# Two mixers of a 256-token network: zero-filled queries, gates and output products with tokens on the partitions, tanh gates on ScalarE

## The chip, the cores and the metric

One core of one Trainium2 chip runs the whole program. The metric is the device time of one execution in microseconds (us). Engines: PE is TensorE, DVE is VectorE, ACT is ScalarE, POOL is GpSimd, SP is SyncE, which here issues the weight loads.

## The reference

256 tokens of width 1024 in fp32 pass through two halves of two layers each. The change touches the mixer that stands in the middle of each of the last two layers:

```python
u = rms_norm_2(h, norm_mix[i])
q, k, v, c, g = jnp.split(u @ w_in[i], splits, axis=-1)   # 512, 128, 128, 1024, 2048
q = rms_norm_2(q.reshape(B, S, 8, 64), q_norm[i])
k = rms_norm_2(k.reshape(B, S, 2, 64), k_norm[i])
y_attn = window_attention(q, k, v, sink[i], rel_bias) @ w_attn_out[i]
c_val, c_gate = jnp.split(c, 2, axis=-1)
c = depthwise_conv(c_val * jax.nn.sigmoid(c_gate), conv_w[i], conv_b[i])   # 31 taps
c = jax.nn.silu(layer_norm_2(c, conv_ln_g[i], conv_ln_b[i]))
y_conv = c @ w_conv_out[i]
g_attn, g_conv = jnp.split(jax.nn.sigmoid(g), 2, axis=-1)
h = h + (g_attn * y_attn + g_conv * y_conv) @ w_o[i]
```

Before and after the mixer stand feed-forward layers (1024 to 2 x 2816 and back), which the change does not touch.

## The kernel before

Activations lie as [feature, token]: 128 features on the partitions, 256 tokens in the free dimension. The weights come as a stream of blocks of 128x2048 (1 MB), in a ring of four slots. SP loads a block (L402), ACT rounds it to fp32r as `whi` (`split_hi`, L480), DVE writes the remainder as `wlo` (`split_lo`, L1102), and PE multiplies in three products: hi x hi, hi x lo, lo x hi (`mm3`, L1985). Each engine's queue is written out by hand and runs in order; all ties between engines are semaphores. A slot is loaded again when PE's `blk_done` says that its block is done.

`window(l)` is the mixer, and each engine has its own function of this name (ACT L937, DVE L1771, PE L2502). Its 24 blocks are:

- blocks for q (2), k, v; after them six fp32 matmuls take the mean square of each head (L2518), ACT forms the inverse root (L966 Ln, L971 Exp), DVE scales q and k (L1822) in six instructions.
- twelve blocks j = 0 to 11: 0 to 3 the convolution's values and gates, 4 to 7 the first gate `g_attn`, 8 to 11 `g_conv`. PE does block j into one of two banks of `ab` (`a_block`, L1999, 48 matmuls with 256 columns), then `attend` for head j - 1 (L2381): scores (L2393) of head j - 1, transposes (L2402) of head j - 2, values (L2421) of head j - 3. I call this a round.
- DVE in round j takes the bank with 1/rms of the tokens applied (`scaled_evac`, L1509), splits the weight block j + 2, finds the row maximum of the scores (`top`, L1659), forms 1/sum (`normal`, L1673) and does 6 or 7 convolution taps, each in two instructions (L1792).
- ACT in round j splits block j + 2, scales the exponentials of head j - 2 by 1/sum (L835, PE's transposes wait for this), then takes the exponentials of head j - 1 (L844) and copies transposed ones (L858). In rounds 1 and 3 it takes a sigmoid of the convolution's gate (L975). The other gates are sigmoids of 2048 columns at once (L982, L987).
- two blocks of `w_attn_out` and two of `w_conv_out` (`b_block`, L2084: 48 matmuls with 256 columns, weights stationary, result as [feature, token] in the four banks of `acc`). Within the first stands the matmul for the convolution's variance (L2541). DVE multiplies the banks by the gates (L1864, L1881), adds the two (L1883), ACT rounds the sum (L1013) and DVE writes its remainder (L1876).
- four blocks of `w_o`, the last two together (`b_last`, L2104), which need the split of both.

`window_attention`'s queries of two heads share a tile, so that a head's queries and keys take 64 of 128 partitions (L2522). `qk` gives per head and query block one fp32 product, which PE runs as two instructions, and two fp32r products with the position bias (L2523 to L2525).

## Time and profile before

| | |
|---|---|
| runs | 2342.78 us median of 3 (2340.3 to 2346.83) |
| profiled execution | span 2338.6 us from first to last instruction; what lies around it is not in the profile |
| PE | 2249.4 us busy, 96% |
| DVE | 1761.8 us, 75% |
| ACT | 1191.4 us, 51% |
| POOL | 236.7 us, 10% |
| chain that ended last | PE 79%, DVE 11%, ACT 5%, DMA 3% |
| DMA | 202 GB/s mean |
| mean granted TensorE clock | 0.990 |

The first mixer lies at about 1344 to 1526 us, the second at about 1934 to 2116. In a timeline a row gives the start, how long until the last of its instructions ended, the engine, the line, output and inputs, shape and count; a bracket gives the idle time before it and who ended it. A matmul's own time contains its way through the array, so that successive ones overlap: the distance of starts is what a matmul costs.

### The profile page before, as it was taken

To read this page: it belongs to the slowest core of one execution; us is meant where nothing else is said; L and a number is where in the kernel's file an instruction comes from. 1 tells how busy PE (TensorE), PEld (TensorE's weight loads), DVE (VectorE), ACT (ScalarE), POOL (GpSimd) and SP (SyncE) were. 2 spreads that over 40 slices of the span, in tenths; PEclk is the share of its full clock that TensorE was granted. 3 is DMA by queue.
4 is the path that set the end of the run, shared out by engine and by line. 5 is a ranking of instruction groups with operands and counts; after the bars stand their busy time and mean duration, and the time that the engine had idled before them with its cause. 6 is when DMAs were issued, how large, how long until landed. Compare 5 with 4: busy or idle time off the path is not lost.

```text
span 2338.6 us, 36936 instructions
## 1 busy us (share of the span) xinstructions
PE 2249.4 (96%) x14724; PEld 2036.4 (87%) x14724; DVE 1761.8 (75%) x1858; ACT 1191.4 (51%) x1293; POOL 236.7 (10%) x199
## 2 busy tenths in 40 slices
PE   7999889999999989999999999999999999999999
PEld 7997889788889877788788998988998899898899
DVE  6898786788789985868677569877577746987755
ACT  3444645455455445555455455655455545565544
POOL 0122000001111300000022000012002200001200
PEclk9999999999999999999999999999999999999999
DMA  9996434577569852455555443455545554344553
GB/s 377 359 351 230 164 124 148 203 266 291 217 257 360 309 194 96 175 180 217 188 183 194 162 162 109 163 181 196 180 170 182 192 180 152 117 146 180 188 188 131
DMA packets 75935, 471.49 MB, mean 202 GB/s; under 512 B 8708, under 2 KB 8964, under 8 KB 27581
## 3 DMA queue, kind: packets, MB, share of 16 engines
q1 hardware_dynamic: 53136, 383.80, 45.2%
q0 software_dynamic: 18976, 68.71, 7.8%
q10 hardware_dynamic: 3724, 17.57, 2.0%
q8 instruction: 74, 1.21, 0.2%
q14 instruction: 25, 0.20, 0.0%
HBM read 468.98 MB, written 1.06 MB: 201 GB/s over the span
## 4 chain that ended last, share of the span: by engine, by line
PE 79%; DVE 11%; ACT 5%; DMA 3%; issue 2%; ACTq 0%; DVEq 0%; SPq 0%
PE ab L1992 19%; PE acc L1992 13%; PE acc L2133 11%; PE mb L2025 10%; PE ab L2025 10%; PE mb L2027 5%; PE ab L2027 5%; DVE wlo L1102 3%; ACT whi L480 2%; PE mb L2393 2%; DMA sc<-start 1%; DMA modmem<-mods 1%; DMA raw<-stream 1%; DVE sc L1792 1%; DVE sc L1241 1%
## 5 line engine op out<-in xcount | busy, mean ns | idle before, releaser
L1102 DVE TENSOR_TENSOR wlo<-raw,whi 128x2048 fp32r<-128x2048 f32 x361 | 832.6, 2310 | 245.2 <-ACT whi L480 242.6
L480 ACT ACTIVATE whi<-raw 128x2048 fp32r<-128x2048 f32 x361 | 689.3, 1911 | 414.0 <-DMA raw<-stream 292.0
L1992 PE MATMUL ab<-uu,whi 128*128 128x256 f32 x3104 | 576.4, 288 | 17.4 <-DVE wlo L1102 8.3
L1992 PEld LDWEIGHTS ab<-uu,whi 128*128 128x128 f32 x3104 | 492.8, 195 | 27.8 <-issue 15.4
L1992 PE MATMUL ab<-uu,wlo 128*128 128x256 f32 x1552 | 443.7, 286 | 0.0
L2025 PE MATMUL ab<-uu,whi 128*128 128x512 f32 x1056 | 374.8, 398 | 8.3 <-DVE uu L1453 5.3
L2025 PE MATMUL mb<-uu,whi 128*128 128x512 f32 x1056 | 375.0, 398 | 3.5 <-DVE wlo L1102 2.1
L1992 PEld LDWEIGHTS ab<-uu,wlo 128*128 128x128 f32 x1552 | 302.7, 195 | 0.0
L1992 PE MATMUL acc<-h_hi,whi 128*128 128x256 f32 (+1 forms) x1032 | 293.4, 284 | 4.4 <-ACT sc L916 1.6
L2027 PE MATMUL ab<-uu,wlo 128*128 128x256 f32 x1056 | 295.6, 280 | 0.0
L2027 PE MATMUL mb<-uu,wlo 128*128 128x256 f32 x1056 | 295.3, 280 | 0.0
L1992 PE MATMUL acc<-h_lo,whi 128*128 128x256 f32 (+1 forms) x1032 | 292.0, 283 | 0.0
L1992 PE MATMUL acc<-h_hi,wlo 128*128 128x256 f32 (+1 forms) x1032 | 292.0, 283 | 0.0
L2025 PEld LDWEIGHTS ab<-uu,whi 128*128 128x128 f32 x1056 | 199.1, 188 | 57.4 <-issue 8.6
L2025 PEld LDWEIGHTS mb<-uu,whi 128*128 128x128 f32 x1056 | 198.8, 188 | 53.5 <-DVE wlo L1102 3.6
L454 POOL TENSOR_TENSOR sc<-sc,rstd 128x512 f32<-128x512 f32 x44 | 120.3, 2733 | 959.2 <-ACT sc L699 959.2
L1992 PEld LDWEIGHTS acc<-h_hi,whi 128*128 128x128 f32 x1032 | 197.4, 191 | 6.2 <-DVE h_lo L1876 2.0
L2027 PEld LDWEIGHTS ab<-uu,wlo 128*128 128x128 f32 x1056 | 200.0, 189 | 0.0
L2027 PEld LDWEIGHTS mb<-uu,wlo 128*128 128x128 f32 x1056 | 199.7, 189 | 0.1
L1992 PEld LDWEIGHTS acc<-h_lo,whi 128*128 128x128 f32 x1032 | 197.4, 191 | 0.1
L1992 PEld LDWEIGHTS acc<-h_hi,wlo 128*128 128x128 f32 x1032 | 197.4, 191 | 0.0
L435 POOL DMA_DIRECT2D modmem<-mods x128 | 68.5, 536 | 939.6 <-DVE sc L1238 658.8
(355 smaller groups left out, 2832.4 us busy)
## 6 DMA issues: line engine op xcount, KB each, us to landing
raw<-stream SPq DMA_DIRECT2D x365, 1024.0 KB, 4.8
modmem<-mods POOLq DMA_DIRECT2D x128, 512.0 KB, 6.0
sc<-lnrows ACTq DMA_DIRECT2D x5, 1024.0 KB, 4.8
sc<-start ACTq DMA_DIRECT2D x4, 1024.0 KB, 16.5
gateb<-gaterows ACTq DMA_DIRECT2D x6, 512.0 KB, 3.8
hank<-toep POOLq DMA_DIRECT2D x8, 192.0 KB, 4.0
x<-xT ACTq DMA_DIRECT2D x1, 1024.0 KB, 27.3
x<-xn ACTq DMA_DIRECT2D x1, 1024.0 KB, 8.8
```

The source lines that it names most:

```text
L435: pool.dma_start(modmem[:, i % MODRING, :], mods[i]).then_inc(mod_in[i % MODRING], 16)
L454: nc.gpsimd.tensor_tensor(gated, gated, r, ALU.mult).then_inc(g2_ready, 1)
L480: nc.scalar.activation(whi[:, n % RAW, :], raw[:, n % RAW, :], ACT.Copy).then_inc(hi_ready, 1)
L1102: nc.vector.tensor_tensor(wlo[:, n % RAW, :], raw[:, n % RAW, :], whi[:, n % RAW, :].bitcast(F32), ALU.subtract).then_inc(lo_ready, 1)
L1241: nc.vector.scalar_tensor_tensor(out=out, in0=part, scalar=cact[:, k:k + 1], in1=out, op0=ALU.mult, op1=ALU.add).then_inc(mod_done, 1)
L1792: ins = nc.vector.scalar_tensor_tensor(out=sc[:, 28 + c, :], in0=cpad[:, c, t:t + T], scalar=w, in1=sc[:, 28 + c, :], op0=ALU.mult, op1=AL ...
L1992: ins = nc.tensor.matmul(out, l, r, start=first and i == 0, stop=last and i == 2, skip_group_check=True)
L2025: nc.tensor.matmul(bank[:, m, :].rearrange("p (a t) -> p a t", a=2), wh[:, k, m * P:m * P + P], uu[:, :, k, :], start=k == 0, stop=k == DM ...
L2027: ins = nc.tensor.matmul(bank[:, m, 0:T], wl[:, k, m * P:m * P + P], u_hi[:, k, :], start=False, stop=k == DM - 1, skip_group_check=True)
L2133: ins = nc.tensor.matmul(acc[:, 2 * t + c, :], l, w[:, k, 512 * c:512 * c + 512], start=first and k == 0 and w is wh and l is hh, stop=las ...
L2393: ins = nc.tensor.matmul(mb[:, k % 2, o:o + w], l, r, start=(c == 0), stop=(c == len(terms) - 1), skip_group_check=True)
```

## The change

1. Queries: DVE writes them into `qpad`, eight tiles of all 128 partitions in the memory of `h_hi`, of which POOL has set everything to zero before; the other head's half stays zero, and the product uses all rows.
2. The gate blocks j = 4 to 11 are done with u stationary (`t_block`), so that the result is [token, feature], and ACT takes it from the bank with tanh, whose scale is half of 1/rms as a column. sigmoid(x) = (1 + tanh(x/2))/2; the 1 is added where DVE multiplies, the half goes into the residual's factor (0.5 for 1.0). The convolution's gates are tanh too.
3. The four blocks of output products are done with the activations stationary and 512 weight columns moving (`quarters`, 24 matmuls a block).
4. The sum of the two, now [token, feature], is turned on PE by 16 transposes in two lots (`turn`), and ACT and DVE take its parts from PSUM.
5. Ln and Exp of the head norms use one table set, and waits on own semaphores become `link`.

```diff
@@ POOL
             for l in range(DEPTH):
                 ffn(4 * l)
+                pool.wait_ge(u_ready, 32 + 16 * l)
+                nc.gpsimd.memset(qpad[:], 0.0).then_inc(qpad_zero, 1)
                 ffn(4 * l + 2)
@@ ACT, window
+                nc.scalar.activation(small[:, 10:12], mb[:, 0, 0:2], ACT.Copy, scale=0.5).then_inc(rcol_ready, 1)
...
                     if j == 0:
+                        nc.scalar.preload_act_table_set("natural_log_exp_and_others")
...
                     elif j in (1, 3):
                         act.wait_ge(bank_evac[a[0] % 2], a[0] // 2 + 1)
-                        nc.scalar.activation(gated, gated, ACT.Sigmoid).then_inc(csig_ready, 1)
+                        nc.scalar.activation(gated, gated, ACT.Tanh, scale=0.5).then_inc(csig_ready, 1)
+                    elif j >= 4:
+                        done(g[0])
+                        i, c = (j - 4) // 4, (j - 4) % 4
+                        for t in range(2):
+                            ins = nc.scalar.activation(gates(i)[:, t, T * c:T * c + T], ab[:, a[0] % 2, t * T:t * T + T],
+                                                       ACT.Tanh, scale=small[:, 10 + t:11 + t])
+                        ins.then_inc(bank_evac[a[0] % 2], 1)
                     tick()
                     if j >= 1:
                         attend(8 + 8 * l, j - 1, 1.0, l)
-                    if j == 9:
...
-                        nc.scalar.activation(sc[:, 0:8, :], sc[:, 0:8, :], ACT.Sigmoid).then_inc(sig_ready, 1)
...
-                gate_sigmoids()
                 split_hi(g[0] + 1 + AHEAD)
                 for q in range(4):
-                    act.wait_ge(comb_ready, 4 * l + q + 1)
-                    nc.scalar.activation(h_hi[:, 8 + 2 * q:10 + 2 * q, :], sc[:, 2 * q:2 * q + 2, :], ACT.Copy)\
+                    act.wait_ge(combt_ps, 4 * l + q + 1)
+                    nc.scalar.activation(h_hi[:, 8 + 2 * q:10 + 2 * q, :], v2(combt(q)), ACT.Copy)\
                         .then_inc(combhi_ready, 1)
@@ DVE, window
-                    else:
-                        scaled_evac(sc[:, 2 * (j - 4):2 * (j - 4) + 2, :])
...
-                        for i in range(6):
...
+                        for b in range(2):
+                            r = slice(64 * b, 64 * b + 64)
+                            ins = nc.vector.scalar_tensor_tensor(out=padded[r, :, b, :], in0=sc[r, 16:20, :],
+                                                                 scalar=small[r, 0:1], in1=sc[r, 32:36, :],
+                                                                 op0=ALU.mult, op1=ALU.mult)
...
+                comb(0)
+                comb(1)
+                comb(2)
+                comb_lo(0)
+                comb_lo(1)
+                comb(3)
+                comb_lo(2)
                 comb_lo(3)
@@ PE, window
                 def qk(h, qb):
-                    r = slice(64 * (h % 2), 64 * (h % 2) + 64)
-                    return [(sc[r, 16 + h // 2, qb * P:qb * P + P], sc[r, 20 + h // 4, :], 0, T),
+                    return [(qpad[:, h, qb * P:qb * P + P], sc[:, 20 + h // 4, :], 0, T),
...
                 for j in range(1, 12):
-                    a_static(1)
+                    if j < 4:
+                        a_static(1)
+                    else:
+                        t_block()
...
+                def turn(c):
+                    pe.wait_ge(comb_ready, 4 * l + 2 * c + 2)
+                    for m in range(4 * c, 4 * c + 4):
+                        for t in range(2):
+                            ins = nc.tensor.transpose(combt(m // 2)[:, T * (m % 2) + P * t:T * (m % 2) + P * t + P],
+                                                      gates(0)[:, t, P * m:P * m + P], ident)
+                        if m % 2:
+                            ins.then_inc(combt_ps, 1)
+
+                quarters(g[0], 0, True, False, None, lambda q: variance() if q == 3 else None)
+                quarters(g[0] + 1, 2, False, True)
...
+                quarters(g[0] + 2, 4, True, False, (m1_ready, 4 * l))
...
+                quarters(g[0] + 3, 6, False, True, None, lambda q: turn(0) if q == 3 else None)
 
                 for i in range(2):
                     pe.wait_ge(comblo_ready, 4 * l + i + 1)
...
+                    if i == 0:
+                        turn(1)
```

How it moves instructions. ACT, a round of the gate blocks (L835 or L849 is the scaling that PE's transposes wait for, L844 or L858 the exponentials, L858 or L872 the copy), before:

```order
L480 ACTIVATE whi<-raw 128x2048
L835 ACTIVATE sc<-sc,small 128x256 x2
L844 ACTIVATE sc,small<-mb,small 128x256 x2
L848 ACTIVATE small<-small,par 128x2
L858 ACTIVATE sc<-acc 128x512
```

and now:

```order
L494 ACTIVATE whi<-raw 128x2048
L994 ACTIVATE sc<-ab,small 128x256 x2
L849 ACTIVATE sc<-sc,small 128x256 x2
L858 ACTIVATE sc,small<-mb,small 128x256 x2
L862 ACTIVATE small<-small,par 128x2
L872 ACTIVATE sc<-acc 128x512
```

The two gate functions (L994), which wait for the round's block, stand ahead of the scaling.

DVE, from the three weight splits behind the first gate products to the next weight splits (L1881 or L1893 multiplies, L1883 or L1895 adds, L1876 or L1899 writes the remainder), before:

```order
L1102 TENSOR_TENSOR wlo<-raw,whi 128x2048 x3
L1881 TENSOR_TENSOR sc<-acc,sc 128x512
L1883 TENSOR_TENSOR sc<-sc 128x512
L1881 TENSOR_TENSOR sc<-acc,sc 128x512
L1883 TENSOR_TENSOR sc<-sc 128x512
L1876 TENSOR_TENSOR h_lo<-sc,h_hi 128x512
L1881 TENSOR_TENSOR sc<-acc,sc 128x512
L1883 TENSOR_TENSOR sc<-sc 128x512
L1876 TENSOR_TENSOR h_lo<-sc,h_hi 128x512
L1881 TENSOR_TENSOR sc<-acc,sc 128x512
L1883 TENSOR_TENSOR sc<-sc 128x512
L1876 TENSOR_TENSOR h_lo<-sc,h_hi 128x512 x2
```

and now:

```order
L1112 TENSOR_TENSOR wlo<-raw,whi 128x2048 x3
L1893 SCALAR_TENSOR_TENSOR sc<-sc,acc 128x512
L1895 TENSOR_TENSOR sc<-sc 128x512
L1893 SCALAR_TENSOR_TENSOR sc<-sc,acc 128x512
L1895 TENSOR_TENSOR sc<-sc 128x512
L1893 SCALAR_TENSOR_TENSOR sc<-sc,acc 128x512
L1895 TENSOR_TENSOR sc<-sc 128x512
L1899 TENSOR_TENSOR h_lo<-ab,h_hi 128x512 x2
L1893 SCALAR_TENSOR_TENSOR sc<-sc,acc 128x512
L1895 TENSOR_TENSOR sc<-sc 128x512
L1899 TENSOR_TENSOR h_lo<-mb,h_hi 128x512 x2
L1112 TENSOR_TENSOR wlo<-raw,whi 128x2048 x3
```

The first remainder stands behind the third sum, and the last two, which read transposed parts, stand right ahead of the next splits.

PE, the end of the second `w_conv_out` block (L2155) and the start of the first `w_o` block (L2014), now:

```order
L2155 MATMUL acc<-wlo,h_hi 128x512
L2155 MATMUL acc<-whi,h_lo 128x512
L2583 MATMUL ab<-par,sc 128x128 x8
L2155 MATMUL acc<-whi,h_hi 128x512
L2155 MATMUL acc<-wlo,h_hi 128x512
L2155 MATMUL acc<-whi,h_lo 128x512
L2155 MATMUL acc<-whi,h_hi 128x512
L2155 MATMUL acc<-wlo,h_hi 128x512
L2155 MATMUL acc<-whi,h_lo 128x512
L2014 MATMUL acc<-h_hi,whi 128x256
```

Eight transposes (L2583) have come in ahead of the last quarter; eight more follow the first `w_o` block.

## Rows read from the trace of the kernel before

**Rows 1.** The page, part 1: busy time, share, instructions.

```profile
PE 2249.4 (96%) x14724; PEld 2036.4 (87%) x14724; DVE 1761.8 (75%) x1858; ACT 1191.4 (51%) x1293; POOL 236.7 (10%) x199
```

**Rows 2.** Timeline, PE, one round: start us, us, engine, line, tiles, form.

```profile
1433.12 0.70 PE L2393 MATMUL mb<-sc 64*128 64x256 f32 x2
...
1435.14 0.60 PE L2402 MATMUL acc<-par,sc 128*128 128x128 f32 x4
1435.67 1.08 PE L2421 MATMUL acc<-sc 128*64 128x256 f32 x4
1436.68 0.51 PE L1992 MATMUL ab<-uu,whi 128*128 128x256 f32 x2
...
1442.63 0.70 PE L2393 MATMUL mb<-sc 64*128 64x256 f32 x2
```

**Rows 3.** Timeline, DVE: first and last of the five rounds 4 to 8.

```profile
1414.57 0.68 DVE L1512 TENSOR_TENSOR sc<-ab,rstd 128x512 f32<-128x512 f32 x1
...
1447.10 2.46 DVE L1792 SCALAR_TENSOR_TENSOR sc<-sc,par 128x256 f32<-128x256 f32 x6
...
1462.69 0.68 DVE L1512 TENSOR_TENSOR sc<-ab,rstd 128x512 f32<-128x512 f32 x1
```

**Rows 4.** Timeline, ACT, one of those rounds.

```profile
1447.23 0.47 ACT L844 ACTIVATE sc<-mb,small 128x256 f32<-128x256 f32 x1 [5.23 <-DVE small L1663]
...
1450.62 0.90 ACT L835 ACTIVATE sc<-sc,small 128x256 f32<-128x256 f32 x2
```

**Rows 5.** Timeline, ACT, DVE and PE, from the head norms to head 1.

```profile
1378.45 1.28 ACT L971 ACT_TABLE_LOAD   x1
1381.45 1.67 DVE L1822 SCALAR_TENSOR_TENSOR sc<-sc,small 128x256 f32<-128x256 f32 x4
1383.97 0.95 PE L2393 MATMUL mb<-sc 64*128 64x256 f32 x2 [1.68 <-DVE sc L1822]
1394.92 0.69 DVE L1512 TENSOR_TENSOR sc<-ab,rstd 128x512 f32<-128x512 f32 x1 [1.48 <-PE ab L1992]
1406.58 0.66 PE L2402 MATMUL acc<-par,sc 128*128 128x128 f32 x4 [1.28 <-ACT sc L835]
1478.51 1.21 DVE L1842 SCALAR_TENSOR_TENSOR sc<-mb,sc 128x1024 f32<-128x1024 f32 x1
```

**Rows 6.** Stretches: engine busy times, granted clock (third number from the end), DMA.

```profile
855.80:859.80 4.00, 3.94 (x33) 3.97 (x34) 3.90 (x6) 3.56 (x5) 0.00 (x0) 1.00 0.43 128
871.30:875.30 4.00, 3.96 (x22) 3.96 (x23) 3.96 (x3) 0.00 (x0) 0.00 (x0) 0.62 0.38 158
...
1384.00:1391.00 7.00, 7.00 (x26) 5.54 (x27) 6.62 (x14) 4.63 (x9) 0.00 (x0) 0.52 0.33 136
```

**Rows 7.** Timeline, PE: two long waits, the first right behind eight transposes.

```profile
852.77 1.20 PE L2260 MATMUL acc<-par,x 128*128 128x128 f32 x8 [0.39 <-DVE x L1401]
855.86 0.36 PE L1992 MATMUL ab<-uu,whi 128*128 128x256 f32 x1 [1.89 <-DVE uu L1357]
...
871.34 0.51 PE L1992 MATMUL ab<-uu,whi 128*128 128x256 f32 x2 [2.88 <-DVE wlo L1102]
```

**Rows 8.** Timeline, PE: 512-column matmuls, then fp32 ones at full height.

```profile
933.13 0.62 PE L2133 MATMUL acc<-whi,h_hi 128*128 128x512 f32 x2
...
1373.80 1.89 PE L2518 MATMUL mb<-sc,par 128*128 128x256 f32 x8
```

**Rows 9.** Timeline, PE, DVE and ACT, from the convolution's variance to the last blocks.

```profile
1482.05 0.70 PE L2541 MATMUL mb<-sc,mean_r 128*128 128x256 f32 x2 [1.21 <-DVE sc L1846]
1489.10 1.28 DVE L1864 TENSOR_TENSOR sc<-acc,sc 128x512 f32<-128x512 f32 x2
1492.10 4.49 DVE L1102 TENSOR_TENSOR wlo<-raw,whi 128x2048 fp32r<-128x2048 f32 x2
1502.47 0.38 PE L1992 MATMUL acc<-h_hi,whi 128*128 128x256 f32 x1 [0.80 <-DVE h_lo L1876]
1506.24 3.71 ACT L480 ACTIVATE whi<-raw 128x2048 fp32r<-128x2048 f32 x2
```

More of the change, by code:

```diff
@@ L1856, in window @@
                 ph[0] += 1
-                dve.wait_ge(sig_ready, 6 * l + 1)
-                for q in range(4):
+                for b in range(2):
+                    dve.wait_ge(bank_evac[b], a[0] // 2)
+                for q, (t, c) in enumerate(QUARTERS):
                     if q % 2 == 0:
@@ L1863, in window @@
                     acc_wait(q)
-                    ins = nc.vector.tensor_tensor(sc[:, 2 * q:2 * q + 2, :], v2(acc[:, q, :]), sc[:, 2 * q:2 * q + 2, :],
-                                                  ALU.mult)
-                    ins.then_inc(m1_ready, 1)
+                    part = gates(0)[:, t, 512 * c:512 * c + 512]
+                    nc.vector.scalar_tensor_tensor(out=part, in0=part, scalar=1.0, in1=acc[:, 2 * t + c, :],
+                                                   op0=ALU.add, op1=ALU.mult).then_inc(m1_ready, 1)
                 split_lo(g[0] - 1 + AHEAD)
@@ L1871, in window, with comb @@
                 ph[0] += 1
-                dve.wait_ge(sig_ready, 6 * l + 2)
+                def comb(q):
+                    t, c = QUARTERS[q]
+                    part, other = [gates(i)[:, t, 512 * c:512 * c + 512] for i in range(2)]
+                    acc_wait(q)
+                    link(nc.vector.scalar_tensor_tensor(out=other, in0=other, scalar=1.0, in1=acc[:, 2 * t + c, :],
+                                                        op0=ALU.add, op1=ALU.mult))
+                    nc.vector.tensor_tensor(part, part, other, ALU.add).then_inc(comb_ready, 1)
                 def comb_lo(q):
                     dve.wait_ge(combhi_ready, 4 * l + q + 1)
-                    nc.vector.tensor_tensor(h_lo[:, 8 + 2 * q:10 + 2 * q, :], sc[:, 2 * q:2 * q + 2, :],
+                    nc.vector.tensor_tensor(h_lo[:, 8 + 2 * q:10 + 2 * q, :], v2(combt(q)),
                                             h_hi[:, 8 + 2 * q:10 + 2 * q, :].bitcast(F32), ALU.subtract).then_inc(comblo_ready, 1)
-                for q in range(4):
-                    acc_wait(q)
-                    link(nc.vector.tensor_tensor(sc[:, 8 + 2 * q:10 + 2 * q, :], v2(acc[:, q, :]),
-                                                 sc[:, 8 + 2 * q:10 + 2 * q, :], ALU.mult))
-                    nc.vector.tensor_tensor(sc[:, 2 * q:2 * q + 2, :], sc[:, 2 * q:2 * q + 2, :],
-                                            sc[:, 8 + 2 * q:10 + 2 * q, :], ALU.add).then_inc(comb_ready, 1)
-                    if q:
-                        comb_lo(q - 1)
+                comb(0)
[5 more added lines that the diff above has]
+                comb_lo(2)
                 comb_lo(3)
@@ L2541, in variance, with quarters @@
                     nc.tensor.matmul(mb[:, 1, 0:T], meanones, sc[:, 36, :], start=True, stop=True).then_inc(cvar_ps, 1)
-                b_block(g[0], h_hi, h_lo, 0, None, True, False, None, variance)
-                b_block(g[0] + 1, h_hi, h_lo, 2, None, False, True)
+                def quarters(n, i, first, last, taken=None, before=None):
+                    split_ready(n)
+                    for q, (t, c) in enumerate(QUARTERS):
+                        if before is not None:
+                            before(q)
+                        if taken is not None:
+                            pe.wait_ge(taken[0], taken[1] + q + 1)
+                        ins = group(n, h_hi, h_lo, i, t, (c,), first, last)
+                        if last and q < 3:
+                            ins.then_inc(acc_done, 1)
+                    ins.then_inc(blk_done, 1)
@@ L2546, in window @@
+                quarters(g[0] + 1, 2, False, True)
                 pe.wait_ge(clo_ready, 2 * l + 1)
-                b_block(g[0] + 2, h_hi, h_lo, 4, None, True, False, (m1_ready, 4 * l))
+                quarters(g[0] + 2, 4, True, False, (m1_ready, 4 * l))
                 pe.wait_ge(clo_ready, 2 * l + 2)
-                b_block(g[0] + 3, h_hi, h_lo, 6, None, False, True)
+                for b in range(2):
+                    pe.wait_ge(bank_evac[b], a[0] // 2)
+                quarters(g[0] + 3, 6, False, True, None, lambda q: turn(0) if q == 3 else None)
```

53 lines of the change are left out of this document (28 added, 25 removed).

## The prediction

> **What bounds the kernel now.** I read the page's shares first: PE is busy 96% of the span [rows 1], and the chain that ended last is mostly PE. So only PE's own work and its few waits count. Then I went through the timelines of PE, DVE and ACT over the first of the two mixers (1344 to 1526 us) and compared the second: its waits on PE are the same ones, of 1.7, 1.3, 1.2 and 0.8 us. All that follows is worked for one mixer and doubled.
>
> In the middle stage PE does one block of the input product and one head per round. A round takes 9.51 us: 2.02 us for the scores, 0.53 for the transposes, 1.01 for the values and 5.95 for the block with its switches [rows 2]. The block has 48 matmuls, so 0.12 us each. DVE is as full as PE: its five rounds 4 to 8 take 48.1 us, 9.62 each, with no idle time [rows 3]. ACT has time: the scaling of a head's exponentials ends at 1451.5 [rows 4], before the block behind which PE wants them is done. The reader is to see that two engines pace this stage, so that taking work from one gives what the other allows, and that ACT, which has slack, is about to get work in a place where PE waits for what is behind it.
>
> **Up to head 2.** The head norms lose a table load of 1.28 us between Ln and Exp. DVE's six products of 256 columns (four take 1.67 us, so 0.4 each, 2.4 in all) become one of 512 and two of 1024 elements per row; a 1024-element product took 1.21 us and issues the next after 1.13, so 2.86 in all [rows 5]. Net: PE's wait of 1.68 us [rows 5] shrinks by 0.8. It is followed now by a stretch of 7 us at a granted clock of 0.52, near the lower of the two levels, 1.2 GHz [rows 6], which makes the second block 3.4 us late, and DVE waits 1.48 us for it [rows 5]. With a wait of 0.9 us and scores that use all rows I take the clock to stay up. DVE then runs on, 0.8 + 1.5 = 2.3 us earlier. That is all this part can give, because head 1's scaling on ACT stands behind a gate function that waits for DVE's fourth evacuation (the 1.28 us wait at 1406.58 [rows 5]). PE, which is faster now, waits there some 4.3 us instead of 1.3. After an idle time of 2.88 us [rows 7] the clock was 0.62 over 4 us [rows 6]; I take the clock to fall at 4.3 us, for 1.7 to 3.4 us, most likely 2.3. **This part: 0**, between -2.3 (no fall) and +1.1.
>
> **Rounds 4 to 8.** Full-height queries replace 64-row ones. Fp32 matmuls at full height issue every 0.216 us (1.89 us for eight, less the last one's 0.38 [rows 8]). A head has four of these and four at 0.12, 1.34 us, and some 0.1 for the switch of format: 1.44 for 2.02. A bound from the other side is nothing saved. The zero rows cost no time of their own; the zeroing is one POOL instruction after 1350 us, where POOL is idle, and its result is needed at 1381. Gates as [token, feature] keep 48 matmuls of 256 columns, so 0.12 us each as before. DVE loses an evacuation of 0.60 us a round, so 9.0 is its pace. But ACT now has, behind its wait for the block, two tanh of 256 columns (an exponential of 256 took 0.47 us [rows 4]; I estimate 0.8 for both, as they overlap) and only then the scaling of the head before (two in 0.90 us [rows 4]), for which PE's transposes wait. From the block's end: 0.2 + 0.8 + 0.9 = 1.9 us, where the scores end after 1.44. So PE waits 0.5 a round, and a round is 1.9 + 0.53 + 1.01 + 5.86 = 9.3. **Five rounds: -1.0**, between -2.5 (DVE's pace) and 0.
>
> In round 9 there are no scores to hide it: PE waits the whole 1.9 us at head 7's transposes, where it waited for nothing. **+1.9**, at least +0.5.
>
> A rule speaks against the first term. In the trace, two 64-row fp32 matmuls take 0.63 us to the next instruction [rows 2], and two at full height 0.43 [rows 8]. The Trainium skill, "TensorE: Matmul & The Clock Gate", section "Step-by-step: what each phase is for", says that a weight load's time goes by columns and that the number of rows does not matter. By that rule the padding would save nothing, and the five rounds would be worth about 0 and not -1.0. The two rows differ with it, and I go by the rows.
>
> **Convolution's variance.** After block 11 PE had the mean (0.6 us) and 36 matmuls of 0.12 to do and then waited 1.21 us [rows 9]: 6.1 us. DVE's last evacuation leaves that chain, but two tanh (0.2 + 0.8) and a weight split (1.9, half of the row at 1506.24 [rows 9]) now stand before ACT's square, which takes 1.1, and DVE's two sums, 1.1: 5.1 us. **-1.0.** From there to the end of DVE's first product at 1489.8 (the row at 1489.10 [rows 9]) the chain goes through ACT and DVE as before, so that the 0.3 us that each block of 24 matmuls of 512 columns saves (0.62 less 0.39 = 0.227 us each [rows 8], 5.44 for 5.76) is not seen here.
>
> **The sum and its transpose.** Counting from that first product's end at 1489.8: DVE has 2.4 us of products and 6.6 of splits (two in 4.49 [rows 9]), then two sums of 1.32 us: done at +11.7. PE has done its block and three quarters of the next at +9.6, so it waits 2.1 us for the sums, then does eight transposes (0.53 for four [rows 2], 1.06) and the last quarter, 1.4. The first output block starts at +14.2; it started at 1502.47, +12.7 [rows 9]. **+1.5.** The wait of 0.80 there [rows 9] goes. Behind that block stand eight more transposes, 1.2 us with the switch. ACT's last two copies wait for them, and the two weight splits that stood at 1506.24 [rows 9] now stand behind the copies. From the block's end: copies done at 1.8 (0.7 for four transposes, then 0.55 each), first split at 3.7, DVE's two splits of 2.2 behind it at 8.15. PE, after 1.2 and a block of 5.76, is there at 6.9. PE waits 1.25 more. **+2.4.**
>
> **Sum:** 0 - 1.0 + 1.9 - 1.0 + 1.5 + 2.4 = +3.8 us a mixer, +8 us in all. Against the profiled span of 2338.6 us that is 2346.6. The median of the runs lies 4.2 over this span, so I forecast 2351 us. A measurement can tell about 0.3%, 7 us. With the bounds above, this case reaches from 2345 to 2355.
>
> **Rivals.**
> *The stalls are smaller and the kernel stays level* (25%): rounds at DVE's 9.0 us, no fall of the clock after the 4.3 us wait. For it: falls don't follow every wait; an idle 1.89 us behind eight transposes [rows 7] left the clock at 1.00 [rows 6]. Against: 4.3 us is longer than any wait inside the trace. Per mixer -2.3 - 1.5 from the sum, 0: 2343 us.
> *Faster: PE's savings go through* (14%). If DVE's rounds can be absorbed by the two spare banks and ACT's tanh is early enough, each mixer keeps 0.6 x 8 of the scores, 1.3 of the wide blocks and the 3.4 us of the lost clock, less 2.1 of transposes: -7.4, so 2328 us. It decides if PE isn't held at head 1's transposes. Against it: DVE without idle time [rows 3].
> *Slower still: the clock falls at the sum, too* (21%). The wait of 2.1 us stands right before eight transposes. A mixer loses 1.7 to 3.4 us there, and perhaps as much at round 9's wait: 2355 to 2361. The rows are divided: 0.62 after 2.88 us of idle, 1.00 after transposes and 1.89 [rows 6, 7]. The Trainium skill, same page, section "Part 4: PE-mode transpose", says that transposes don't count as work for the clock; by this rule the fall here is sure.
> *The change doesn't do what it says* (under 2%, in the first rival): the order of PE's instructions shows it does.
>
> **How the numbers follow.** Forecast 40%, level 25%, slower still 21%, faster 14%. Slower by over 0.3% is above 2350: 60% of the forecast and the third rival, 0.45. Faster is 0.15, the rest is same. For 8 in 10 the range leaves out the faster case and the top of the third rival: 2338 to 2358.
>
> **What would show it.** Steps right: a PE wait of about 4 us for ACT's scaling before head 1's transposes with a clock under 1 after it; waits of about 0.5 us in rounds 4 to 8 and 1.9 in round 9, all on that line; 2 us before the first eight transposes, released by DVE's sum; 1.2 us before the last two blocks, released by DVE's split. Wrong: rounds of 9.0 us or less, no wait before the transposes of the sum, or a mixer (first block to last) shorter than now.

## The result and the profile after

| | before | the change |
|---|---|---|
| median of 18 runs each | 2342.97 us | 2352.0 us |
| ratio | 1 | 1.0032 (95%: 1.0025 to 1.0040) |
| profiled execution, span | 2338.6 us | 2350.7 us |
| from the head norms to the end of the last `w_o` block, first and second mixer | 151.8, 151.8 us | 154.8, 157.5 us |

The change makes the kernel slower by 9 us. The last line is taken from PE's timeline: from the first `headones` matmul (L2518, now L2540) to the first matmul behind the mixer. I call it the mixer's length; every experiment below is judged by it first, because the code outside the mixers, which is the same, differs by some us from execution to execution. Of the 12.1 us between the two profiled spans 3.0 and 5.6 lie in the mixers, 1.3 ahead of them and 2.1 between them, where every matmul of 110 us took a little longer. A profile of another execution of the changed kernel has 156.7 and 156.8 us. The mean of the four is 156.45, so 4.6 us a mixer, 9.3 in all: this accounts for the medians.

The page's first part shows PE as busy as before [rows 1], and DVE and ACT relieved by 6 and 11 us:

```profile
PE 2248.5 (96%) x14564; PEld 2034.6 (87%) x14564; DVE 1756.0 (75%) x1836; ACT 1180.5 (50%) x1311; POOL 240.3 (10%) x201
```

The time is in waits. Timeline of the changed kernel, PE, first mixer (start us, us, engine, line, tiles, form; in brackets the idle time before the row and what ended it):

```profile
1384.80 0.70 PE L2415 MATMUL mb<-sc,qpad 128*128 128x256 f32 x2 [1.18 <-DVE qpad L1835]
...
1391.99 0.60 PE L2415 MATMUL mb<-sc,qpad 128*128 128x256 f32 x2
...
1393.33 0.60 PE L2424 MATMUL acc<-par,sc 128*128 128x128 f32 x4
...
1405.69 1.11 PE L2424 MATMUL acc<-par,sc 128*128 128x128 f32 x4 [4.68 <-ACT sc L849]
...
1416.60 0.66 PE L2424 MATMUL acc<-par,sc 128*128 128x128 f32 x4 [0.39 <-ACT sc L849]
...
1425.94 0.66 PE L2424 MATMUL acc<-par,sc 128*128 128x128 f32 x4 [0.39 <-ACT sc L849]
...
1463.22 0.66 PE L2424 MATMUL acc<-par,sc 128*128 128x128 f32 x4 [1.72 <-ACT sc L849]
...
1482.63 0.70 PE L2565 MATMUL mb<-sc,mean_r 128*128 128x256 f32 x2 [0.31 <-DVE sc L1861]
...
1502.07 1.09 PE L2583 MATMUL ab<-par,sc 128*128 128x128 f32 x8 [1.75 <-DVE sc L1895]
...
1518.33 0.36 PE L2014 MATMUL acc<-h_hi,whi 128*128 128x256 f32 x1 [1.41 <-DVE wlo L1112]
```

Against [rows 5, 9] the wait ahead of the first scores is down from 1.68 to 1.18 us, that ahead of the variance from 1.21 to 0.31, and that ahead of the first `w_o` block is gone. Head 1's went from 1.28 to 4.68, and four places are new: 0.39 in each of rounds 4 to 8, 1.72 in round 9, 1.75 at the sum's transposes, 1.41 at the last blocks. A head's scores now take 1391.99 to 1393.33, 1.34 us, against 2.02 [rows 2].

The same stretch on ACT shows who holds PE. L989 is the convolution's gate, L994 the other gates, L849 the scaling for which PE waits:

```profile
1404.21 0.63 ACT L989 ACTIVATE sc<-sc 128x512 f32<-128x512 f32 x1 [2.90 <-DVE sc L1522]
1404.75 0.89 ACT L849 ACTIVATE sc<-sc,small 128x256 f32<-128x256 f32 x2
...
1414.92 0.84 ACT L994 ACTIVATE sc<-ab,small 128x256 f32<-128x256 f32 x2 [3.42 <-PE ab L2014]
1415.65 0.90 ACT L849 ACTIVATE sc<-sc,small 128x256 f32<-128x256 f32 x2
```

ACT is idle for 2.90 and 3.42 us with the scaling's inputs ready (DVE's `normal` had ended at 1400.4), because the gate function stands ahead of it.

Stretches of the changed kernel (busy times of PE, PEld, DVE, ACT, POOL; then granted clock, DMA share, GB/s):

```profile
1404.00:1409.00 5.00, 3.31 (x9) 1.84 (x10) 4.93 (x8) 2.42 (x8) 0.00 (x0) 0.67 0.02 5
1464.00:1468.00 4.00, 4.00 (x30) 3.46 (x29) 3.65 (x7) 2.32 (x2) 0.00 (x0) 1.00 0.48 199
1502.00:1506.00 4.00, 3.93 (x28) 3.68 (x29) 3.88 (x7) 1.09 (x2) 0.00 (x0) 1.00 0.14 16
2099.00:2102.00 3.00, 3.00 (x11) 2.51 (x10) 1.98 (x3) 1.19 (x2) 0.00 (x0) 0.50 0.00 0
```

The fall behind the first scores [rows 6] is gone. The clock falls behind the 4.68 us wait instead, not behind the waits of 1.72 and 1.75 in the first mixer, but behind the second mixer's wait at the sum (1.88 us), to 0.50 over 2099 to 2102.

### The profile page after: what moved, and what is told of

It is laid out like the page before. It is cut to its first block, busy times and chain, and to the rows that moved or that the text cites. A ratio compares the mean times of both kernels' runs of the same rounds, so it can differ in the third digit from the quotient of the medians.

```text
span 2350.7 us, 36614 instructions
## 1 busy us (share of the span) xinstructions
PE 2248.5 (96%) x14564; PEld 2034.6 (87%) x14564; DVE 1756.0 (75%) x1836; ACT 1180.5 (50%) x1311; POOL 240.3 (10%) x201
## 4 chain that ended last, share of the span: by engine, by line
PE 79%; DVE 11%; ACT 5%; DMA 2%; issue 2%; ACTq 0%; DVEq 0%; SPq 0%
PE ab L2014 19%; PE acc L2014 13%; PE acc L2155 13%; PE mb L2047 10%; PE ab L2047 10%; PE mb L2049 5%; PE ab L2049 5%; DVE wlo L1112 3%; ACT whi L494 1%; DMA sc<-start 1%; DMA modmem<-mods 1%; DVE sc L1803 1%; PE acc L2443 1%; DVE sc L1251 1%; PE acc L2424 1%
## 5 line engine op out<-in xcount | busy, mean ns | idle before, releaser
L2014 PE MATMUL ab<-uu,whi 128*128 128x256 f32 x2592 | 479.6, 287 | 17.1 <-DVE wlo L1112 8.3
L2014 PEld LDWEIGHTS ab<-uu,whi 128*128 128x128 f32 x2592 | 411.0, 195 | 21.6 <-issue 10.9
L2014 PE MATMUL ab<-uu,wlo 128*128 128x256 f32 x1296 | 370.2, 286 | 0.0
L2049 PE MATMUL ab<-uu,wlo 128*128 128x256 f32 x1056 | 296.7, 281 | 0.0
L2014 PE MATMUL acc<-h_hi,whi 128*128 (+1 forms) x904 | 256.4, 284 | 5.6 <-DVE wlo L1112 2.8
L2014 PE MATMUL acc<-h_lo,whi 128*128 (+1 forms) x904 | 255.8, 283 | 0.0
L2014 PE MATMUL acc<-h_hi,wlo 128*128 (+1 forms) x904 | 255.8, 283 | 0.0
L2014 PEld LDWEIGHTS ab<-uu,wlo 128*128 128x128 f32 x1296 | 252.5, 195 | 0.0
L2047 PEld LDWEIGHTS ab<-uu,whi 128*128 128x128 f32 x1056 | 199.5, 189 | 57.9 <-issue 8.5
L2049 PEld LDWEIGHTS ab<-uu,wlo 128*128 128x128 f32 x1056 | 200.6, 190 | 0.0
L2014 PEld LDWEIGHTS acc<-h_hi,whi 128*128 128x128 f32 x904 | 173.5, 192 | 7.0 <-issue 3.9
L2155 PE MATMUL acc<-whi,h_hi 128*128 128x512 f32 x512 | 173.0, 394 | 1.6 <-DVE wlo L1112 0.8
L2014 PEld LDWEIGHTS acc<-h_lo,whi 128*128 128x128 f32 x904 | 173.5, 192 | 0.1
L2014 PEld LDWEIGHTS acc<-h_hi,wlo 128*128 128x128 f32 x904 | 173.5, 192 | 0.0
```

Source lines behind the costliest of these rows:

```text
L2014: ins = nc.tensor.matmul(out, l, r, start=first and i == 0, stop=last and i == 2, skip_group_check=True)
L2047: nc.tensor.matmul(bank[:, m, :].rearrange("p (a t) -> p a t", a=2), wh[:, k, m * P:m * P + P], uu[:, :, k, :], start=k == 0, stop=k == DM ...
L2049: ins = nc.tensor.matmul(bank[:, m, 0:T], wl[:, k, m * P:m * P + P], u_hi[:, k, :], start=False, stop=k == DM - 1, skip_group_check=True)
L2155: ins = nc.tensor.matmul(acc[:, 2 * t + c, :], l, w[:, k, 512 * c:512 * c + 512], start=first and k == 0 and w is wh and l is hh, stop=las ...
```

## The experiments

Two theories stood against each other. *ACT's order and the late sum*: PE is held where the prediction has it, by gate functions ahead of the scaling, by the sums and by the late splits. *DVE's pace*: DVE is as full as PE, so a freed wait only comes back as one for DVE.

In the table, parts of a mixer in us, on PE: from the first scores to head 3's; from there to head 7's scores (four rounds); to head 7's transposes; to the variance; the mixer's length. Two figures are the two mixers.

| kernel | to h3 | four rounds | to its transposes | to variance | length | median us, ratio (95%) |
|---|---|---|---|---|---|---|
| before | 30.15 | 38.01 | 9.42 | 20.50 | 151.8 | 2343 |
| the change | 29.92, 30.86 | 37.30 | 11.20 | 19.4 | 154.8, 157.5 | 2352.0, 1.0032 |
| the change, again | 30.21, 30.34 | 37.3 | 11.21 | 20.9 | 156.7, 156.8 | 2354.3, 1.0046 (1.0029 to 1.0062) |
| gates behind | 30.88, 31.12 | 34.9 | 8.73 | 19.4 | 150.9, 151.1 | 2340.5, 0.9988 (0.9978 to 0.9998) |
| conv gate behind | 24.81 | 40.4 | 11.20 | 20.95, 19.43 | 154.4, 152.9 | 2344.1, 1.0011 (1.0000 to 1.0022) |
| both behind | 24.81 | 37.2 | 10.6 | 19.4 | 149.1, 149.0 | 2338.6, 0.9985 (0.9973 to 0.9996) |
| turn early | 30.80, 30.62 | 37.3 | 11.20 | 19.4 | 154.0, 153.8 | 2347.4, 1.0027 (1.0016 to 1.0039) |
| all moves | 24.80 | 37.2 | 10.6 | 19.4 | 145.7, 145.7 | 2332.0, 0.9955 (0.9942 to 0.9968) |
| all moves, again | 24.81 | 37.2 | 10.6 | 19.4 | 145.7, 145.7 | 2331.4, 0.9946 (0.9932 to 0.9960) |
| all moves, 64 rows | 25.66 | 38.0 | 9.42 | 19.4 | 146.1, 146.1 | 2335.5, 0.9974 (0.9960 to 0.9988) |

**Gates behind the scaling** (rounds of j = 4 to 11, on ACT; `mid` takes the two tanh with it):

```diff
-                    elif j >= 4:
-                        done(g[0])
...
                     tick()
-                        attend(8 + 8 * l, j - 1, 1.0, l)
+                        attend(8 + 8 * l, j - 1, 1.0, l, mid)
@@ attend
                     ins.then_inc(p_norm, 1)
+                if mid is not None:
+                    mid()
```

> The changed kernel, with ACT's two gate tanh of a round (j = 4 to 11) issued behind the scaling of the exponentials that PE's transposes wait for. Theory ACT order (the prediction's): the PE waits of 0.39 us in rounds 4 to 8 and of 1.72 us in round 9 go, rounds fall from 9.32 to DVE's pace of about 9.0 us, so 1.6 + 1.7 = 3.3 us a mixer: span about 2344, ratio to before about 1.0005. Rival DVE pace: DVE is the bound already and hands PE a new wait of the same size (for the conv sums or a weight split): under 1 us a mixer, ratio stays at 1.003.

Measured: every 0.39 and the 1.72 are gone, as ACT's order predicts, and nothing on DVE took their place. Timeline of this kernel, PE:

```profile
1406.26 1.12 PE L2432 MATMUL acc<-par,sc 128*128 128x128 f32 x4 [4.68 <-ACT sc L849]
...
1416.25 0.59 PE L2423 MATMUL mb<-sc,qpad 128*128 128x256 f32 x2
...
1424.99 0.60 PE L2423 MATMUL mb<-sc,qpad 128*128 128x256 f32 x2
...
1459.92 0.60 PE L2432 MATMUL acc<-par,sc 128*128 128x128 f32 x4
```

Rounds are 8.74 us (1416.25 to 1424.99), and not DVE's 9.0: PE is late after head 1, so DVE is ahead of it (it waits 1.25 us for PE's scores at 1417.79), and PE runs at its own pace, busy for all of the 52 us from 1408 to 1460. The two parts that this edit touches, the four rounds and the one to head 7's transposes, get shorter by 2.4 and 2.5 us, 4.8 together, not 3.3. This order in ACT's queue alone costs as much as the whole change (4.6). The mixer's length is 5.4 us under the change's mean; the rest lies in the falls of the clock, which differ from mixer to mixer (none here behind round 9 or at the sum, longer ones behind head 1).

**The convolution's gate behind** (the same with j = 3 alone; with j = 1 `mid` is called at once):

```diff
-                    elif j in (1, 3):
-                        act.wait_ge(bank_evac[a[0] % 2], a[0] // 2 + 1)
-                        nc.scalar.activation(gated, gated, ACT.Tanh, scale=0.5).then_inc(csig_ready, 1)
+                    if j in (1, 3):
+                        def mid(ai=a[0]):
+                            act.wait_ge(bank_evac[ai % 2], ai // 2 + 1)
+                            nc.scalar.activation(gated, gated, ACT.Tanh, scale=0.5).then_inc(csig_ready, 1)
```

> The changed kernel, with only the tanh of the convolution's second gate (j = 3) issued behind the scaling of head 1. Theory ACT order: PE's wait of 4.68 us before head 1's transposes shrinks to about 1.2 us, and the granted clock of 0.50 behind it goes; PE gains 3.5 us or more there, but DVE's round 3 (1403.5 to 1413.7, no idle time) does not move, so that only the small rounds' slack is won: 1 to 3 us a mixer. Rival clock: the fall costs most of the loss, and with it gone the mixer gains 4 us or more, ratio at or under 1.000. Rival DVE pace: nothing is won, ratio 1.003, the wait shows up again on a row released by DVE.

PE, first mixer, and two stretches:

```profile
1402.91 0.65 PE L2432 MATMUL acc<-par,sc 128*128 128x128 f32 x4 [1.14 <-ACT sc L849]
1413.83 0.66 PE L2432 MATMUL acc<-par,sc 128*128 128x128 f32 x4 [1.97 <-ACT sc L849]
```

```profile
1401.00:1406.00 5.00, 3.86 (x25) 2.89 (x25) 4.99 (x11) 2.49 (x4) 0.00 (x0) 1.00 0.65 213
1414.00:1418.00 4.00, 4.00 (x19) 3.15 (x19) 3.96 (x7) 0.38 (x2) 0.00 (x0) 0.65 0.21 86
```

The wait is 1.14 us and no fall follows it. The part up to head 3 shrinks by 5.5 us to 24.81, but the four rounds grow by 3.1: head 2 now waits 1.97 us, with a fall of the clock behind it. So 2.8 us a mixer are kept, within the theory's 1 to 3; here neither rival holds. This part also prices the fall after 4.68 us. Without it the part would have been 24.81 + (4.68 - 1.14) = 28.35. The eight mixers with the wait of about 4.7 us have 29.92 to 31.12, mean 30.6: the fall costs 1.6 to 2.8 us, 2.2 in the mean. This takes the part to be the same otherwise.

**Both behind.**

> Both of these orders together (j = 3 to 11). Theory ACT order: DVE sets the pace from round 3 on, 9.0 us a round; at most 1 us a mixer more than the first of them alone gives: 3.3 to 4.3 us a mixer, span 2342 to 2344. Rival clock: the two add up, 7 us or more a mixer, span under 2337.

149.0 us, 7.4 less than the change, and a span of 2333.2: not the 3.3 to 4.3 of the theory, but the 7 and more that I had given the rival, near the sum of the two orders (5.4 + 2.8 = 8.2). I had put too little on the clock: in this kernel no wait inside the rounds is over 1.6 us and the clock does not fall in either mixer of this profile, which neither order alone gave. DVE's pace shows up now: the last rounds are 8.9 to 9.1 us, and heads 1, 2 and 7 wait 1.1 to 1.5 us.

**The turn early** (DVE's third weight split goes behind the fourth sum):

```diff
                 split_lo(g[0] - 1 + AHEAD)
                 split_lo(g[0] + AHEAD)
-                split_lo(g[0] + 1 + AHEAD)
...
                 comb(3)
+                split_lo(g[0] - 1 + AHEAD)
                 comb_lo(2)
```

> The changed kernel with DVE's third weight split moved from ahead of the first sum to behind the fourth. Theory: the sums are no longer late, PE's wait of 1.75 us before the first eight transposes shrinks to about 0.2, and the clock does not fall there in either mixer: 1.6 us a mixer, 3.3 us in all and 1 to 2 us more where the clock fell; ratio 1.001 to 1.002. Rival acc pace: the second sum waits for PE's second quarter anyway, and the wait stays above 1 us, ratio 1.003.

PE's transposes and the DVE row that releases them, this kernel:

```profile
1496.67 1.09 PE L2583 MATMUL ab<-par,sc 128*128 128x128 f32 x8
...
1512.92 0.36 PE L2014 MATMUL acc<-h_hi,whi 128*128 128x256 f32 x1 [1.41 <-DVE wlo L1112]
```

```profile
1493.84 0.69 DVE L1892 SCALAR_TENSOR_TENSOR sc<-sc,acc 128x512 f32<-128x512 f32 x1 [0.45 <-PE acc L2155]
```

No wait is left at the transposes, DVE even waits 0.45 us for PE's first quarter, and from the variance to the first `w_o` block it takes 20.1 us in both mixers for 21.8. The wait of 1.41 at the last blocks is untouched. Both were as expected. The median ratio (1.0027) does not lie clear of the change's two (1.0032 and 1.0046); what the move gives, 1.6 us a mixer, is read from this part alone. The remaining 0.9 us against the change's mean length lies in the falls of the clock, of which none stands behind round 9 or at the sum here.

**All moves**: both orders, the turn early, and the split of the third `w_o` block ahead of the last two copies and remainders:

```diff
@@ ACT
                         .then_inc(combhi_ready, 1)
+                    if q == 1:
+                        split_hi(g[0] + 2 + AHEAD)
...
-                b_blocks(4)
+                b_blocks(4, 1)
@@ DVE
+                split_lo(g[0] + AHEAD)
                 comb_lo(2)
                 comb_lo(3)
-                b_blocks(4)
+                b_blocks(4, None, 1)
```

> Both orders on ACT, and in the output part two moves: DVE's third weight split goes from ahead of the first sum to behind the fourth, and on both engines the split of the third w_o block goes ahead of the last two copies (ACT) and remainders (DVE) of the turned sum. Expected beside what the two ACT orders give: the 1.75 us wait before the first eight transposes shrinks to 0.3, with it the clock fall behind it in the second mixer (1.6 us), and the 1.41 us wait before the last two blocks goes: 2.9 us a mixer and 1.6 once. Theory: 2 x (3.3 to 4.3) + 2 x 2.9 + 1.6 = 14 to 16 us under the change, 2336 to 2338, ratio 0.997 to 0.998: faster than both. Rival DVE pace: DVE's moved splits come late for PE elsewhere, ratio 1.000 or above.

> The version with all four moves once more, beside the one with POOL's taps: 145.7 us a mixer, ratio 0.995 to 0.996, no stretch of a mixer at a granted clock under 0.9.

The last stretch (first `w_o` block to the end) goes from 25.5 to 23.9 us, the one before it from 21.8 to 20.1. All of PE's waits over 0.2 us that are left in the first mixer, and the clock in three stretches of it:

```profile
1384.93 0.70 PE L2426 MATMUL mb<-sc,qpad 128*128 128x256 f32 x2 [1.18 <-DVE qpad L1845]
1402.28 0.66 PE L2435 MATMUL acc<-par,sc 128*128 128x128 f32 x4 [1.14 <-ACT sc L849]
1412.46 0.66 PE L2435 MATMUL acc<-par,sc 128*128 128x128 f32 x4 [1.24 <-ACT sc L849]
1457.56 0.66 PE L2435 MATMUL acc<-par,sc 128*128 128x128 f32 x4 [1.51 <-ACT sc L849]
1476.98 0.70 PE L2576 MATMUL mb<-sc,mean_r 128*128 128x256 f32 x2 [0.31 <-DVE sc L1871]
1484.86 0.47 PE L2166 MATMUL acc<-whi,h_hi 128*128 128x512 f32 x1 [0.33 <-DVE sc L1891]
```

```profile
1375.00:1415.00 40.00, 36.45 (x268) 33.68 (x267) 36.08 (x67) 20.79 (x36) 0.00 (x0) 1.00 0.38 132
1415.00:1470.00 55.00, 53.27 (x391) 47.61 (x390) 54.61 (x117) 31.38 (x64) 0.00 (x0) 1.00 0.31 115
1470.00:1520.00 50.00, 49.22 (x318) 44.22 (x317) 40.85 (x41) 28.15 (x32) 0.00 (x0) 1.00 0.42 148
```

145.7 us in all four mixers of two profiles, 6.1 less than before: with its queues ordered for it, the change makes the kernel 11 us **faster** than before (ratios 0.9955 and 0.9946) and 20 us faster than the change as it was made. I had expected 0.997 to 0.998; the two orders on ACT gave the surplus. In the middle stretch DVE is busy 54.61 of 55 us, PE 53.27.

**64 rows again**, in the changed kernel and in the version with all moves:

```diff
-                    return [(qpad[:, h, qb * P:qb * P + P], sc[:, 20 + h // 4, :], 0, T),
+                    r = slice(64 * (h % 2), 64 * (h % 2) + 64)
+                    return [(qpad[r, h, qb * P:qb * P + P], sc[r, 20 + h // 4, :], 0, T),
```

> The changed kernel with scores over 64 rows again (the queries' 64 rows of the padded tile by the keys' 64), all else as changed. Theory rows as traced: a head's scores take 2.02 us and not 1.34; the first three are hidden in the 4.68 us wait before head 1's transposes, the five in rounds 4 to 8 take up the 0.39 us wait and lengthen the round by 0.3: 1.5 us a mixer, 3 us in all, ratio 1.0045. Rival, the rule that the row count costs nothing: scores stay at 1.34 us and the ratio at 1.003.

> The version with all four moves (149.0 - 3.3 = 145.7 us from the head norms to the mixer's end) with 64-row scores. Theory rows as traced: PE's own round becomes 8.7 + 0.7 = 9.4 us and passes DVE's 9.0, so 0.4 us in each of five rounds and a part of the first three: 2 to 4 us a mixer, 147.7 to 149.7. Rival, the row rule: 145.7 again.

PE in the changed kernel with 64 rows:

```profile
1404.22 0.70 PE L2415 MATMUL mb<-sc,qpad 64*128 64x256 f32 x2
1405.27 0.70 PE L2415 MATMUL mb<-sc,qpad 64*128 64x256 f32 x2
1408.95 1.11 PE L2424 MATMUL acc<-par,sc 128*128 128x128 f32 x4 [2.54 <-ACT sc L849]
```

Half a head's scores take 1.05 us (1404.22 to 1405.27), and a whole head's in a round 2.02, as before, for 1.34 at full height. It is tempting to take this for the price of 64 rows. The trace of the kernel before has short fp32 products in a row, in its first half:

```profile
282.28 1.99 PE L2312 MATMUL acc<-sc 16*128 16x256 f32 x8
...
334.62 1.96 PE L2345 MATMUL acc<-sc 64*128 64x256 f32 x12 [1.21 <-ACT sc L802]
```

Eight with 16 rows take 1.99 us, where eight at full height took 1.89 [rows 8]: the first takes 0.32 us to the next one's start, all others 0.216, as at full height. Twelve with 64 rows, in the two halves of the partitions by turns, take 1.96. So in a run of one height the number of rows costs nothing. The Trainium skill ("TensorE: Matmul & The Clock Gate", "Step-by-step: what each phase is for") says that the number of rows does not matter for a weight load's time. These rows agree with it. The extra time stands where PE goes from one height to another: from a matmul of 128 rows to the first of 16 it is 0.21 us (0.12 between 128-row ones), then the 0.32, and 0.30 from the last 16-row one to the next of 128 and 0.22 behind that. The scores with 64 rows show the same four distances (0.21, 0.32, 0.31, 0.22), in each half of a head, because their 64-row products alternate with the 128-row ones of the position bias. The zero-filled queries save these changes of height.

But little of the 0.7 us arrives. In the changed kernel (155.7 and 157.4 us, the second with three falls of the clock, median 2351.8, ratio 1.0046, 1.0029 to 1.0063) the four rounds go from 37.30 to 38.01, and the first three heads hide in head 1's wait, which shrinks from 4.68 to 2.54 (and to 1.28 in the second mixer, where the clock falls behind the first scores). With all moves, where I expected 2 to 4 us, it is 0.4 a mixer: 0.9 and 0.8 us in the first two parts, of which 1.2 come back at head 7, whose wait of 1.51 is used up. PE's saving on the scores is worth 0.4 us out of 8 x 0.68 = 5.4, because DVE, busy for 87.32 of the 88 us from 1385 to 1473 in the version with all moves, sets the length of this stage. (The medians of the two lie 3.6 us apart, more than the mixers' 0.8; the rest lies outside the mixers and stays open. The profiled span of the 64-row version, 2325.9 us, is even the shorter one.)

**The kernel before, with zero-filled queries alone**, and **with head 1's scaling ahead of the gate besides**:

```diff
+                pool.wait_ge(u_ready, 32 + 16 * l)
+                nc.gpsimd.memset(qpad[:], 0.0).then_inc(kn_ps, 1)
...
-                        for i in range(6):
+                        for b in range(2):
+                            r = slice(64 * b, 64 * b + 64)
+                            ins = nc.vector.scalar_tensor_tensor(out=padded[r, :, b, :], in0=sc[r, 16:20, :],
...
-                    return [(sc[r, 16 + h // 2, qb * P:qb * P + P], sc[r, 20 + h // 4, :], 0, T),
+                    return [(qpad[:, h, qb * P:qb * P + P], sc[:, 20 + h // 4, :], 0, T),
```

> The kernel before with the zero-filled queries alone (POOL's zeroing, DVE's three products for six, full-height scores). Theory two engines pace: scores shrink to 1.34 us, but DVE's rounds of 9.62 us have no idle time, so that PE waits 0.6 us a round for DVE instead: 0 to 1 us a mixer, ratio 0.999 to 1.000. Rival PE pace: 8 x 0.68 = 5.4 us a mixer, ratio 0.995. Rival slower: the products' 0.46 us more on DVE delay the first scores and the fall of the clock behind them lasts longer: up to +1 us a mixer.

> The kernel before with the zero-filled queries, and the sigmoid of the convolution's second gate (j = 3) issued behind head 1's scaling. It tells what the good version (145.7 us a mixer) owes to the order and what to the change itself. Theory DVE pace: before, DVE's work up to the convolution's mean has no idle time but 1.48 us, and its rounds need 9.62 us, so that PE's shorter scores and the freed wait cannot be used: 150 to 152 us a mixer, ratio 0.998 to 1.001. Rival: order and PE's scores are what pays, 147 or less, ratio 0.995.

The first has 152.0 and 154.6 us (median 2349.1, ratio 1.0016, 1.0000 to 1.0032), no gain from 5.4 us less work on PE and rather a loss. PE:

```profile
1385.78 0.70 PE L2402 MATMUL mb<-sc,qpad 128*128 128x256 f32 x2 [2.46 <-DVE qpad L1830]
1406.67 0.55 PE L2411 MATMUL acc<-par,sc 128*128 128x128 f32 x3 [3.18 <-ACT sc L839]
...
1462.60 0.65 PE L2411 MATMUL acc<-par,sc 128*128 128x128 f32 x4 [2.12 <-ACT sc L839]
```

The waits grow to 2.46, 3.18 and 2.12 us, and the clock falls behind the first two in both mixers, behind the third in one: what PE saves it pays in waits and to its clock. With the order mended too (median 2344.7, ratio 1.0009, 0.9998 to 1.0021) the length is 150.7 and 150.6, as DVE's pace has it: DVE is then busy 85.17 of the 86 us from 1387 to 1473. In the second mixer the clock fell behind the 2.46 us wait (0.50 from 1978 to 1981), the next round took 8.71 us for 7.20, and the mixer was no longer for it: PE would have waited for DVE anyway.

So about 1 of the 6.1 us a mixer comes from the queries and the first order. Where the rest lies, in us of the first mixer (before the first scores; the part up to head 3; from there to the variance; from there to the mixer's end):

| kernel | to the first scores | to h3 | h3 to variance | variance to end |
|---|---|---|---|---|
| before | 10.2 | 30.2 | 67.9 | 43.6 |
| before, zero-filled queries and order | 11.0 | 24.8 | 71.4 | 43.6 |
| all moves | 9.7 | 24.8 | 67.3 | 44.0 |

From the second line to the third the head norms, with a table load less, give 1.3, and the stretch that DVE paces, with eight of its evacuations gone, gives 4.1. The output products with 512 columns and the turn give nothing: even with the splits moved, that part is some 0.4 us longer than before. Which share each item has within a part was not tested.

**The change once more.**

> The changed kernel once more: ratio 1.003. For the clock: it falls after the 4.68 us wait before head 1's transposes in both mixers; after the 1.7 to 1.9 us wait before the sum's transposes it falls in both if transposes do not hold it up, and in none or one if what counts there is chance.

Ratio 1.0046, with 1.0032 inside its interval. The clock fell behind head 1's wait and behind round 9's in both mixers, and behind the wait at the sum (1.84 and 1.75 us) in none:

```profile
1404.00:1410.00 6.00, 3.37 (x10) 1.89 (x11) 5.93 (x10) 2.48 (x8) 0.00 (x0) 0.50 0.16 64
1465.00:1468.00 3.00, 3.00 (x12) 1.92 (x11) 2.65 (x7) 2.40 (x2) 0.00 (x0) 0.56 0.70 289
1503.00:1508.00 5.00, 3.16 (x22) 2.85 (x22) 4.88 (x8) 1.09 (x2) 0.00 (x0) 1.00 0.04 18
```

**Taps on POOL**: the good version with eight taps of two channel blocks on POOL.

```diff
+                    op(nc.gpsimd.tensor_scalar(to, cpad[:, c, t:t + T], w, None, ALU.mult))
+                    if i >= 2:
+                        op(nc.gpsimd.tensor_tensor(part, part, to, ALU.add))
...
-            7: ((1, 10, 3), (1, 13, 4)), 8: ((1, 17, 3), (1, 20, 4)), 9: ((1, 24, 2), (1, 26, 2)),
+            7: ((1, 4, 3), (1, 7, 3)), 8: ((1, 10, 3), (1, 13, 3)), 9: ((1, 16, 2), (1, 18, 2)),
```

> The version with all four moves, and of the convolution's taps the last eight of channel blocks 2 and 3 on POOL (a product and a sum each, added by DVE at the end); DVE keeps 6 taps a round for 7 in rounds 2 to 8. In the version with all four moves DVE has no idle time from 1385 to 1473 us. Theory DVE pace: its rounds fall from 9.0 to 8.2 us, PE's own 8.7 us decide, and PE's waits of 1.14, 1.24 and 1.51 us for the scaling of heads 1, 2 and 7 shrink: rounds 4 to 8 lose 0.3 each, head 7 up to 1.5, heads 1 and 2 up to 1.5: 3 to 5.5 us a mixer, from 145.7 to 140 to 143. Rival: POOL's and DVE's operations slow each other or POOL is not done in time, and DVE waits for it in round 11: 145 or more.

149.1 and 148.8 us (median 2335.5, ratio 0.9972, 0.9961 to 0.9983): 3.2 us a mixer worse than without. The rival is right. Six taps on DVE, in the good version, and here beside a POOL operation:

```profile
1416.86 2.46 DVE L1813 SCALAR_TENSOR_TENSOR sc<-sc,par 128x256 f32<-128x256 f32 x6
```

```profile
1414.04 3.95 DVE L1832 SCALAR_TENSOR_TENSOR sc<-sc,par 128x256 f32<-128x256 f32 x6
...
1446.69 2.46 DVE L1832 SCALAR_TENSOR_TENSOR sc<-sc,par 128x256 f32<-128x256 f32 x6
```

While POOL works (1405.6 to some 1442 us) the same six instructions take 2.6 to 3.95 us, and 2.46 again behind it. POOL's products take 0.97 us beside DVE's taps, and 3.09 or 2.84 where they meet a weight split of DVE (1410.99 to 1413.27 and 1422.25 to 1424.74):

```profile
1410.88 3.09 POOL L489 TENSOR_SCALAR ptap<-sc,par 128x256 f32<-128x256 f32 x1
...
1414.89 0.97 POOL L489 TENSOR_SCALAR ptap<-sc,par 128x256 f32<-128x256 f32 x1
```

PE waits up to 1.92 us (2.00 in the second mixer) at heads 3 and 4 for the delayed 1/sum, with a fall of the clock behind it in both. So the test of DVE's pace by relieving DVE did not come off; that DVE's pace holds the good version rests on its 54.61 of 55 us, on the 64-row runs and on the fall that cost nothing in the run above.

## Why the prediction was right

The forecast was 2351, the median 2352.0, and the steps hold one by one; that the two medians lie within 1 us is partly luck, as said below. The two profiles of the change give four mixers.

| step | forecast | measured, us a mixer |
|---|---|---|
| wait before the first scores | -0.8 | -0.5 |
| head 1: wait, then fall of the clock | 4.3, 2.3 | 4.68, 2.2 |
| up to head 3 in all | 0 (-2.3 to +1.1) | -0.7, +0.2, -0.4, -0.3 |
| rounds 4 to 8 | 0.5 wait, 9.3 a round, -1.0 | 0.39, 9.32, -0.9 |
| round 9 | +1.9 | +1.8 |
| variance | -1.0 | -1.1 where the clock stays up |
| sum and its transposes | wait 2.1, +1.5 | 1.75, +1.3 |
| last blocks | wait 1.25, +2.4 | 1.41, +2.4 |

*Up to head 2.* Right in mechanism and in size. DVE's three products took 3.2 us (1381.51 to 1384.7), not 2.86, which is the difference of 0.8 to 0.5. That the clock would stay up behind the first scores, and fall behind head 1's wait, came out in all four mixers. "Net 0" was right to 0.7 us, but as the difference of terms of 3 to 5 us, and by that partly luck.

*Rounds.* The scaling behind two tanh was the cause: moving them behind it took the 0.39 and 1.72 us away. The floor of 9.0 us a round holds only while DVE is not ahead (8.9 to 9.1 with both behind); with the gates alone behind and PE late, rounds ran at 8.74. The first term, the shorter scores, has the right size, but its reason was misread. The prediction set two 64-row fp32 matmuls (0.63 us) against two at full height (0.43) and took the rule on rows to be contradicted. The 0.63 contains the change from and to 128 rows; in a run of one height the rows agree with the rule.

*Sum and last blocks.* The splits ahead of the sums were the cause at the first (turn early), those behind the copies at the second (all moves).

*The rival that the clock falls at the sum, too*, came true in part, mostly at round 9. Ahead of the sum's transposes twelve profiled mixers had a wait of 1.75 to 1.88 us: the clock fell in one. The prediction read the Trainium skill (same page, "Part 4: PE-mode transpose": transposes don't count as work for the clock) so that the fall there is sure; the traces speak against that reading. Behind the 1.72 us wait of round 9 it fell in four of ten, and cost 1.5 us each time. Behind 4.7 us at head 1 it fell in eight of eight. In the change's four mixers there were three such falls, two at round 9 and one at the sum, about 1.2 us a mixer in the mean. Without them the change costs 3.4 us a mixer, a little under my +3.8, and with them 4.6: that the forecast met the median so closely is luck in part, and two executions differ by several us.

*The faster rival* was priced at 7.4 us a mixer and stood under the condition that PE isn't held at head 1's transposes. Once PE is not, and the other three places are mended, the gain is 6.1. The size came near, but not by its terms: the shorter scores, priced at 4.8, are worth 0.4 once the rest is in order, and the output part, priced at 1.3 less 2.1, is 0.4 longer. What carries the gain is the part up to head 3, 5.4 us shorter with the clock up. In the change as made the order on ACT denied it; once that is mended, "DVE without idle time" is the limit.

## What to carry to other kernels

When an engine with slack is given new work in an in-order queue, look at what stands behind that work and who waits for it: here two tanh of 0.8 us, which themselves wait for a block, ahead of a scaling whose inputs were ready turned a gain of some 3 us (gates behind) into a loss of 9. A saving on one of two equally full engines is worth next to nothing until the other is relieved as well, and the freed engine's longer waits can cost it its clock. Mend the order of the queues first, then judge the change.
